# Two mixture-of-experts layers: six weight chunks in flight instead of three, and another order of the expert products

## The chip, the core and the metric

The kernel runs on one core of a Trainium2 chip. The metric is the device time of one execution in microseconds; lower is better. TensorE (PE) multiplies, ScalarE (ACT) and VectorE (DVE) move and transform results, GpSimd (POOL) does one kind of subtraction, and SyncE (SP) issues the loads from device memory (HBM) into the on-chip memory (SBUF). Matmul results land in eight banks of PSUM, here the tensor `bank`.

## What is computed

A model of 256 tokens, 1024 wide: two first blocks (stick-breaking attention or retention, each followed by a mixture-of-experts layer), then a second block (state-space and sparse attention, then a layer that picks from 16384 small experts), all in float32. The change concerns the two mixture-of-experts layers and the weights that they stream:

```python
def grouped_moe(h, router_w, router_b, w_gate, w_up, w_down):
    ...
    for e in range(N_EXPERTS):                       # 16 experts
        hidden = jax.nn.silu(t @ w_gate[e]) * (t @ w_up[e])      # 1024 -> 512
        out = out + combine[:, e:e + 1] * (hidden @ w_down[e])   # 512 -> 1024
```

`combine` is zero except for the two experts that the router chose for a token.

## The kernel before

**Weights.** All weights of the first two blocks and of the mixer lie in one HBM tensor `stream`, in chunks of 128 x 4096 float32 (2 MB). SP loads them in order into `K.ring`, three places (`RING = 3`): chunk n goes to place n % 3, and its load waits until TensorE has used chunk n - 3, counted by the semaphore `chunk_used`. A landed chunk counts on `landed[place]`. SP works through its waits and loads strictly in the order of the program, so each load waits behind the one before it.

**An expert layer** (`moe_stage`, used twice, called `moe0` and `moe1` here) takes two experts, a pair, at a time: 8 pairs, 6 chunks each, 48 chunks a layer. Of the six, two hold the gate weights, two the up weights, two the down weights. At the beginning the layer routes the tokens and gathers each expert's tokens (up to 64) into `slots` with a product by a 0/1 matrix `hot`; `gather(0)` makes the slots of experts 0 to 7, `gather(1)` those of 8 to 15, and `turn_hot` transposes `hot` for the way back. A branch on the router's counts leads to this path (`tensor_gathered`) or to `tensor_dense`; the execution profiled takes the gathered path.

**TensorE's order** in the gathered path: `gather(0)`; gate product of pair 0; `spread_weights`; up product of pair 0; a small product for the output gate; `gather(1)`; `turn_hot`; `turn_hidden(0)`; down product of pair 0. Then for each pair p from 1 to 7: gate product (2 chunks), up product (2 chunks), `scatter` of pair p - 1, `turn_hidden(p)`, down product (2 chunks). At the end `scatter` of pair 7.

**Its partners.** ACT applies Silu to the gate product (bank 4) once both gate chunks are done (`silu_gate`); DVE multiplies it with the up product (bank 5) into `hidden_s` (`make_hidden`); TensorE transposes that into bank 4 (`turn_hidden`); ACT copies it to `hidT` (`take_hidden`), and the down product (banks 6 and 7) waits for the copy. DVE and ACT then split the down product into two parts, `y_hi` and `y_lo` (`split_values`, `take_values`), which `scatter` adds into banks 0 to 3. `y_hi` and `y_lo` lie in `K.halves`, where the tokens' two parts for the gathers had been.

**Other memory.** `K.w_hi` and `K.w_lo` (16 KB a partition each) hold split weights in the retention stage between the two layers; within the expert layers they are idle until the last pair. All instructions of the first products have one line in the profile, L1053; the down products L1094, the gathers L1036, `turn_hot` L1072, `turn_hidden` L1080, `scatter` L1102, SP's chunk loads L1373 in the layers and L149 elsewhere.

## Time and profile before

| | us |
|---|---|
| median of 3 runs | 2084.95 (2083.53 to 2085.63) |
| profiled execution, its own time | 2082.98 |
| its span in the trace | 2081.1 |
| TensorE busy | 1915.7 (92%) |
| weight loads of TensorE busy | 1418.1 (68%) |
| DVE / ACT / POOL busy | 1099.6 / 745.0 / 628.9 |
| read from HBM | 483.41 MB, mean 233 GB/s |

The profiled execution's own time is 1.88 us above its span and 1.97 us below the median of the runs. The busy share of TensorE is an average over stages: matmuls overlap in the pipeline and a stage that waits for its weights stands beside stages that wait for nothing. What decides is, within a stage, which wait ends last.

### The profile page before, as it was taken

How to read it: one execution, taken by the hardware profiler on the slowest of the kernel's cores; microseconds unless marked ns; L12 is line 12 of the kernel's file. 1: busy time of each engine (PE TensorE's matmuls, PEld its weight loads, DVE VectorE, ACT ScalarE, POOL GpSimd, SP SyncE). 2: the span in 40 equal slices, each digit the busy share in tenths (PEclk: the TensorE clock that was granted, in tenths of full speed). 3: DMA queues.
4: the chain of work that ended last, by engine and by line, in shares of the span. 5: the costliest groups of instructions: out<-in, count | busy, mean ns of one | idle time of the engine just before them, and what ended most of it. 6: DMA issues, size and time to landing. Idle time of an engine off the chain costs nothing. (4 is left out here: it accounts for less than half of the span.)

```text
span 2081.1 us, 30590 instructions
## 1 busy us (share of the span) xinstructions
PE 1915.7 (92%) x10508; PEld 1418.1 (68%) x10508; DVE 1099.6 (53%) x2221; ACT 745.0 (36%) x1260; POOL 628.9 (30%) x438
## 2 busy tenths in 40 slices
PE   4989888888999998887999999999999999999998
PEld 4875432237877642222776559999999998888886
DVE  4377210124668621012697521999577776555555
ACT  5362200014354220001512333555544445444444
POOL 6720000016668100000300025898766760000000
PEclk9999999999999899999999999999999999999999
DMA  9874699993668369999332332555444446555554
GB/s 395 311 278 170 242 426 424 427 418 130 230 231 342 123 248 425 413 422 422 106 131 92 132 122 99 174 183 183 162 144 142 144 142 202 191 192 188 190 190 148
DMA packets 76621, 485.54 MB, mean 233 GB/s; under 512 B 9472, under 2 KB 9984, under 8 KB 58624
## 3 DMA queue, kind: packets, MB, share of 16 engines
q1 hardware_dynamic: 75824, 482.88, 61.8%
q10 hardware_dynamic: 720, 1.61, 0.2%
q8 instruction: 50, 0.82, 0.2%
q14 instruction: 27, 0.22, 0.0%
HBM read 483.41 MB, written 1.05 MB: 233 GB/s over the span
## 5 line engine op out<-in xcount | busy, mean ns | idle before, releaser
L3083 POOL TENSOR_TENSOR peer_u_lo<-peer_u,peer_u_hi 128x512 fp32r<-128x512 f32 x255 | 328.2, 1299 | 93.7 <-ACT peer_u_hi L3109 92.1
L3021 PE MATMUL bank<-peer_hn_hi,peer_u_hi 128*128 128x256 f32 x1024 | 294.3, 287 | 3.5 <-ACTq L3096 3.5
L1053 PE MATMUL bank<-ring,moe_slots 128*64 128x512 f32 x1024 | 237.4, 608 | 64.4 <-DMA ring<-in_stream 64.4
L3022 PE MATMUL bank<-peer_hn_lo,peer_u_hi 128*128 128x256 f32 x1024 | 286.6, 280 | 0.0
L3023 PE MATMUL bank<-peer_hn_hi,peer_u_lo 128*128 128x256 f32 x1024 | 286.2, 279 | 0.0
L1053 PEld LDWEIGHTS bank<-ring,moe_slots 128*64 128x64 f32 x1024 | 69.9, 139 | 228.7 <-issue 116.2
L3109 ACT ACTIVATE peer_u_hi<-peer_u 128x512 fp32r<-128x512 f32 x253 | 159.1, 629 | 114.9 <-PE bank L3023 111.2
L3021 PEld LDWEIGHTS bank<-peer_hn_hi,peer_u_hi 128*128 128x128 f32 x1024 | 193.4, 189 | 5.8 <-issue 3.7
L3022 PEld LDWEIGHTS bank<-peer_hn_lo,peer_u_hi 128*128 128x128 f32 x1024 | 193.5, 189 | 0.0
L3023 PEld LDWEIGHTS bank<-peer_hn_hi,peer_u_lo 128*128 128x128 f32 x1024 | 193.2, 189 | 0.0
L217 POOL TENSOR_TENSOR w_lo<-ring,w_hi 128x1024 fp32r<-128x1024 f32 x60 | 148.6, 2478 | 62.7 <-ACT w_hi L207 62.4
L3239 DVE TENSOR_TENSOR peer_v_lo<-peer_scores,peer_v_hi 128x1024 fp32r<-128x1024 f32 x86 | 105.4, 1225 | 102.0 <-ACT peer_v_hi L3129 102.0
L1193 DVE SCALAR_TENSOR_TENSOR moe_hidden_s<-bank,moe_slot_w,moe_gated_s 128x512 f32<-128x512 f32 x16 | 12.0, 749 | 242.7 <-PE bank L1053 242.7
L3129 ACT ACTIVATE peer_v_hi<-peer_scores 128x1024 fp32r<-128x1024 f32 x86 | 91.2, 1061 | 118.6 <-PE bank L3063 112.0
L1094 PE MATMUL bank<-ring,moe_hidT 128*64 128x512 f32 x512 | 117.0, 610 | 14.4 <-ACT moe_hidT L1155 9.6
L3063 PE MATMUL bank<-peer_hn_hi,peer_hn_lo 128*128 128x512 f32 x504 | 121.4, 390 | 0.0
L3063 PEld LDWEIGHTS bank<-peer_hn_hi,peer_hn_lo 128*128 128x128 f32 x504 | 94.6, 188 | 19.6
L1386 POOL TENSOR_TENSOR w_lo<-ring,w_hi 128x1024 fp32r<-128x1024 f32 x4 | 9.5, 2429 | 312.1 <-ACT w_hi L1137 312.1
L322 DVE CUSTOM_DVE_ANT_0 mod<-sb_mod_ring,bank 128x1024 bf16<-128x1024 f32 x64 | 76.7, 1217 | 49.8 <-DMA sb_mod_ring<-in_ada_t 29.3
L207 ACT ACTIVATE w_hi<-ring 128x1024 fp32r<-128x1024 f32 x60 | 63.6, 1060 | 107.2 <-PE bank L246 73.0
L3063 PE MATMUL bank<-peer_v_hi,peer_hn_lo 128*128 128x512 f32 x344 | 100.5, 393 | 0.0
L2044 POOL COPY s_steps<-consts 128x128 f32<-128x128 f32 x1 | 0.3, 293 | 317.9 <-POOLq L115 317.9
(510 smaller groups left out, 3977.8 us busy)
## 6 DMA issues: line engine op xcount, KB each, us to landing
ring<-in_stream SPq DMA_DIRECT2D x135, 2048.0 KB, 10.5
peer_u<-in_peer_u SPq DMA_DIRECT2D x128, 512.0 KB, 3.3
peer_scores<-in_peer_v SPq DMA_DIRECT2D x86, 512.0 KB, 3.3
sb_mod_ring<-in_ada_t SPq DMA_DIRECT2D x64, 512.0 KB, 6.7
peer_u<-in_peer_v SPq DMA_DIRECT2D x42, 512.0 KB, 3.3
ret_mod_ring<-in_ada_t SPq DMA_DIRECT2D x32, 512.0 KB, 5.0
s_bz<-in_b_channel SPq DMA_DIRECT2D x4, 512.0 KB, 6.0
ring<-in_stream SPq DMA_DIRECT2D x2, 1024.0 KB, 5.0
```

Of the source, the lines that this page charges most:

```text
L217: pool.tensor_tensor(self.shaped(self.w_lo, q, by_columns), self.quarter(n, q, by_columns), self.shaped(self.w_hi, q, by_columns).bitcast( ...
L322: dve.tensor_tensor_reduce(out=self.junk[:, b % 2, :], in0=self.ring[:, b % self.slots, :], in1=c_wide, scale=1.0, scalar=0.0, op0=ALU.mul ...
L1053: last = pe.matmul(K.bank[own(e), 4 + up, :], slots[:, f, own(2 * p + e)], w[:, e, k, :], start=(f == 0), stop=(f == KD - 1))
L1094: last = pe.matmul(K.bank[own(e), 6 + dh, :], hidT[:, k, own(e)], w[:, e, k, :], start=(k == 0), stop=(k == 3))
L3021: pe.matmul(out, u_hi[:, b, k2, :], h_hi[:, k, :], start=(k == 0), stop=False)
L3022: pe.matmul(out, u_hi[:, b, k2, :], h_lo[:, k, :], start=False, stop=False)
L3023: last = pe.matmul(out, u_lo[:, b, k2, :], h_hi[:, k, :], start=False, stop=(k == KD - 1))
L3063: last = pe.matmul(K.bank[:, 4 + 2 * tt + dh, :], h[b][:, mine], w[b][:, dh * 512:(dh + 1) * 512], start=first_tile and begins, stop=last_ ...
L3083: pool.tensor_tensor(u_lo[:, b, :, :], u[:, i, KD // 2 * half:KD // 2 * (half + 1), :], u_hi[:, b, :, :].bitcast(F32), ALU.subtract).then_ ...
L3109: act.activation(u_hi[:, b, :, :], u[:, i, KD // 2 * half:KD // 2 * (half + 1), :], ACT.Copy).then_inc(hi_made, 1)
L3129: act.activation(v_hi[i], v[i], ACT.Copy).then_inc(v_ready, 1)
L3239: dve.tensor_tensor(v_lo[i], v[i], v_hi[i].bitcast(F32), ALU.subtract)
```

## The change

The six chunks of a pair get six places. `RING` becomes 4, and in the expert layers two more places, `early`, lie in the memory of `K.w_hi` and `K.w_lo`. Up chunks and (but for the first and last pair) down chunks go through the ring, gate chunks through `early`; the gate chunks of pair 0 come through the ring and the down chunks of pair 7 through `early`. The host lays the chunks out in the order of their use, and `ROW` maps chunk numbers to rows of `stream`. Four chunks of a layer can be in the ring before it begins, and two more are issued as SP's first act in it, ahead of the two rows `g_row` and `b_row`; 42 loads are left for the loop instead of 45. TensorE runs the gate product of pair p + 1 ahead of the down product of pair p, with the transposes of `hidden_s` (now into bank 5) between its two chunks, and `gather(1)` and `turn_hot` come after the up product of pair 1. `y_hi` and `y_lo` get memory of their own. ACT's and DVE's orders follow. The dense path is rewritten for the same chunk order (left out below). A smaller scratch area for GpSimd's loads makes room, and `peer_gap` keeps later buffers off the ring's fourth place.

```diff
--- before.py
+++ after.py
...
-RING = 3
+RING = 4
...
-STREAM = [("sb_in", 6), ("sb_out", 2), ("moe0", 3 * EXPERTS), ("ret_in", 12), ("ret_out", 4), ("moe1", 3 * EXPERTS),
+STREAM = [("sb_in", 6), ("sb_out", 2), ("moe0", 4 * PAIRS), ("ret_in", 12), ("ret_out", 4), ("moe1", 4 * PAIRS),
...
+ROW = []
+_r = 0
+for _name, _count in STREAM:
+    if _name.startswith("moe"):
+        ROW += [_r + 6 * p + m for p in range(PAIRS) for m in range(4)]
+        _r += 6 * PAIRS
+    else:
+        ROW += list(range(_r, _r + _count))
+        _r += _count
+ROWS = _r
...
-        sp.dma_start(K.ring[:, n % RING, 0:size], K.A["stream"][n, :, 0:size]).then_inc(K.landed[n % RING], 16)
+        sp.dma_start(K.ring[:, n % RING, 0:size], K.A["stream"][ROW[n], :, 0:size]).then_inc(K.landed[n % RING], 16)
...
 def weight_buffers(K, scope):
 
+    with ExitStack() as chunks:
+        K.early = chunks.enter_context(K.nc.sbuf_tensor("early", [P, 2, CHUNK], F32))
     K.w_hi, K.w_lo = (scope.enter_context(K.nc.sbuf_tensor(n, [P, 4, CHUNK // 4], F32R)) for n in ("w_hi", "w_lo"))
...
-        y_hi, y_lo = (K.halves[:, 0, i * D:(i + 1) * D] for i in range(2))
+        y_hi, y_lo = (sb(n, [P, D], F32R) for n in ("y_hi", "y_lo"))
...
+        early = [K.early[:, m, :] for m in range(2)]
+        early_landed, early_used = [s_(f"early_in{m}") for m in range(2)], s_("early_used")
+        row0, turn0 = ROW[n0], n0 // RING
+        assert n0 % RING == 0 and n_end % RING == 0
...
+        def chunk(pe, slot, turn):
+
+            pe.wait_ge(K.landed[slot], 16 * (turn + 1) + 16 * turn0)
+            return two_experts(K.ring[:, slot, :])
+
+        def early_chunk(pe, m, turn):
+
+            pe.wait_ge(early_landed[m], 16 * (turn + 1))
+            return two_experts(early[m])
+
+        def gate_chunk(pe, p, m):
+            return chunk(pe, m, 0) if isinstance(p, int) and p == 0 else early_chunk(pe, m, p - 1)
+
+        def down_chunk(pe, p, dh):
+            return early_chunk(pe, dh, PAIRS - 1) if isinstance(p, int) and p == PAIRS - 1 else chunk(pe, dh, p + 1)
+
+        def gate_used(p):
+            return K.chunk_used if isinstance(p, int) and p == 0 else early_used
+
+        def down_used(p):
+            return early_used if isinstance(p, int) and p == PAIRS - 1 else K.chunk_used
+
+        def gated_by(p):
+            return (K.chunk_used, n0 + 2) if isinstance(p, int) and p == 0 else (early_used, 2 * p)
+
+        def downed_by(p, dh):
+            return (early_used, 2 * PAIRS - 1 + dh) if p == PAIRS - 1 else (K.chunk_used, n0 + 4 * p + 5 + dh)
...
+            def gate_product(p, m):
+
+                if p and m == 0:
+                    pe.wait_ge(silu_done, p)
+                first_products(gate_chunk(pe, p, m), p, 0, m).then_inc(gate_used(p), 1)
+
+            def up_product(p):
 
                 for m in range(2):
-                    n = at(p, 2 * up + m)
-                    wait_chunk(pe, K, n)
-                    w = K.ring[:, n % RING, :].rearrange("p (e k c) -> p e k c", e=2, k=4)
-                    for k in range(4):
-                        f = 4 * m + k
-                        if not up and p == 0:
-                            took(0, f)
-                        if not up and p == PAIRS // 2:
-                            took(1, f)
-                        for e in range(2):
-                            last = pe.matmul(K.bank[own(e), 4 + up, :], slots[:, f, own(2 * p + e)], w[:, e, k, :], start=(f == 0),
-                                             stop=(f == KD - 1))
-                    last.then_inc(K.chunk_used, 1)
+                    first_products(chunk(pe, 2 + m, p), p, 1, m).then_inc(K.chunk_used, 1)
...
-                    last = pe.transpose(K.bank[:, 4, k * P:(k + 1) * P], hidden_s[:, k * P:(k + 1) * P], K.ident)
+                    last = pe.transpose(K.bank[:, 5, k * P:(k + 1) * P], hidden_s[:, k * P:(k + 1) * P], K.ident)
...
             gather(0)
             took(0, 2)
-            first_products(0, 0)
+            gate_product(0, 0)
+            gate_product(0, 1)
             spread_weights()
-            first_products(0, 1)
+            up_product(0)
             pe.wait_ge(slot_taken, 2)
             gate.tensor(pe)
+            gate_product(1, 0)
+            turn_hidden(0)
+            gate_product(1, 1)
+            pe.wait_ge(gate.taken, 2)
+            down_product(0)
+            up_product(1)
             gather(1)
             turn_hot()
-            turn_hidden(0)
-            pe.wait_ge(gate.taken, 2)
-            down_product(0)
-            for p in range(1, PAIRS):
-                first_products(p, 0)
-                first_products(p, 1)
-                if p == 1:
-                    pe.wait_ge(copied, 4)
+            gate_product(2, 0)
+            turn_hidden(1)
+            gate_product(2, 1)
+            pe.wait_ge(copied, 4)
+            scatter(0)
+            down_product(1)
+            for p in range(2, PAIRS):
+                up_product(p)
+                if p + 1 < PAIRS:
+                    gate_product(p + 1, 0)
+                turn_hidden(p)
+                if p + 1 < PAIRS:
+                    gate_product(p + 1, 1)
                 scatter(p - 1)
-                turn_hidden(p)
                 down_product(p)
             scatter(PAIRS - 1)
...
+                act.wait_ge(early_used, 2 * PAIRS)
...
-                act.activation(hidT[:].rearrange("p k s -> p (k s)"), K.bank[:, 4, :], ACT.Copy).then_inc(hid_taken, 1)
+                act.activation(hidT[:].rearrange("p k s -> p (k s)"), K.bank[:, 5, :], ACT.Copy).then_inc(hid_taken, 1)
...
+            take_hidden(0)
+            silu_gate(1)
+            take_values(0)
             take_slots(1)
             act.wait_ge(made, 1)
             for b in range(4):
                 act.activation(hotT[:, 2 * b:2 * b + 2, :].rearrange("p a t -> p (a t)"), K.bank[:, b, :], ACT.Copy).then_inc(copied, 1)
-            take_hidden(0)
-            for p in range(1, PAIRS):
+            take_hidden(1)
+            silu_gate(2)
+            for p in range(2, PAIRS):
                 take_values(p - 1)
-                silu_gate(p)
                 take_hidden(p)
+                if p + 1 < PAIRS:
+                    silu_gate(p + 1)
             take_values(PAIRS - 1)
...
                 dve.tensor_copy(slot_w[own(e), :], weights[own(e), :, e]).then_inc(slot_taken, 1)
             dve.wait_ge(slot_taken, 2)
-            take_slots(1)
             make_hidden(0)
...
-            for p in range(1, PAIRS):
+            split_values(0)
+            make_hidden(1)
+            take_slots(1)
+            for p in range(2, PAIRS):
                 split_values(p - 1)
                 make_hidden(p)
...
+                for m in range(2):
+                    sp.dma_start(early[m], K.A["stream"][row0 + 4 + m]).then_inc(early_landed[m], 16)
                 affine_rows(sp, K, 2 * layer, g_row, b_row, rows_in)
-                LOOPS = (n_end - n0 - RING) // RING
-                assert K.fetched == n0 + RING and (n_end - n0) % RING == 0
-                with sp.Fori(0, LOOPS) as i:
-                    for j in range(RING):
-                        slot = (n0 + j) % RING
-                        sp.wait_ge(K.chunk_used, RING * i + (n0 + j + 1))
-                        sp.dma_start(K.ring[:, slot, :], K.A["stream"][RING * i + (n0 + RING + j)]).then_inc(K.landed[slot], 16)
+                assert K.fetched == n0 + RING
+                with sp.Fori(0, PAIRS - 1) as i:
+                    for slot in range(RING):
+                        sp.wait_ge(K.chunk_used, RING * i + (n0 + slot + 1))
+                        sp.dma_start(K.ring[:, slot, :], K.A["stream"][6 * i + (row0 + 6 + slot)]).then_inc(K.landed[slot], 16)
+                    for m in range(2):
+                        sp.wait_ge(early_used, 2 * i + (m + 1))
+                        sp.dma_start(early[m], K.A["stream"][6 * i + (row0 + 10 + m)]).then_inc(early_landed[m], 16)
                 K.fetched = n_end
...
+            peer.enter_context(nc.sbuf_tensor("peer_gap", [P, CHUNK], F32))
...
-    return parts
+    gates, ups, downs = parts[0::3], parts[1::3], parts[2::3]
+    order = [gates[0], ups[0], gates[1]]
+    for p in range(PAIRS):
+        order += [downs[p]] + ups[p + 1:p + 2] + gates[p + 2:p + 3]
+    return order
...
-    nc = bacc.Bacc("TRN2", target_bir_lowering=False, num_devices=1)
+    nc = bacc.Bacc("TRN2", target_bir_lowering=False, num_devices=1, dynamic_dma_scratch_size=1024)
```

TensorE, from `gather(0)` of the first layer to the first `scatter`; `ring` and `early` are the chunk places, `moe_slots` the gathered tokens, `moe_hot` the 0/1 matrix. Before:

```order
L1036 MATMUL bank<-moe_hot,halves 128x512 x32
L1053 MATMUL bank<-ring,moe_slots 64x512 x16
L1062 MATMUL bank<-moe_comb,moe_hot 128x2 x16
L1053 MATMUL bank<-ring,moe_slots 64x512 x16
L356 MATMUL bank<-mod,consts 128x512 x2
L1036 MATMUL bank<-moe_hot,halves 128x512 x32
L1072 MATMUL bank<-consts,moe_hot 128x128 x16
L1080 MATMUL bank<-consts,moe_hidden_s 128x128 x4
L1094 MATMUL bank<-ring,moe_hidT 64x512 x16
L1053 MATMUL bank<-ring,moe_slots 64x512 x32
L1102 MATMUL bank<-halves,moe_hotT 128x512 x8
```

The same stretch of the changed kernel, whose line numbers are other ones (L1081 gathers, L1094 first products, L1144 down products):

```order
L1094 MATMUL bank<-ring,moe_slots 64x512 x16
L368 MATMUL bank<-mod,consts 128x512 x2
L1094 MATMUL bank<-early,moe_slots 64x512 x8
L1132 MATMUL bank<-consts,moe_hidden_s 128x128 x4
L1094 MATMUL bank<-early,moe_slots 64x512 x8
L1144 MATMUL bank<-ring,moe_hidT 64x512 x16
L1094 MATMUL bank<-ring,moe_slots 64x512 x16
L1081 MATMUL bank<-moe_hot,halves 128x512 x32
L1124 MATMUL bank<-consts,moe_hot 128x128 x16
L1094 MATMUL bank<-early,moe_slots 64x512 x8
L1132 MATMUL bank<-consts,moe_hidden_s 128x128 x4
```

Six more chunks' products (two gate, two down, two up) now stand between the first up product and the second gather. One `order` row of x16 is two chunks, of x8 one chunk.

SP in the first layer, from its first load there to the end of its loop. Before:

```order
L522 DMA mod<-in_ln_g 128x1024
L523 DMA moe_b_row<-in_ln_b 128x1024
L1369 UNCONDITIONAL_BRANCH
L1369 ISA
L1373 ISA
L1373 DMA ring<-in_stream 128x4096
L1372 REGISTER_ALU
L1373 ISA
L1373 DMA ring<-in_stream 128x4096
L1373 ISA
L1373 DMA ring<-in_stream 128x4096
```

Of the changed kernel, the loads ahead of the loop and the last of its body, with the loads for the next stage behind it:

```order
L1433 DMA early<-in_stream 128x4096 x2
L534 DMA mod<-in_ln_g 128x1024
L535 DMA moe_b_row<-in_ln_b 128x1024
...
L1442 DMA early<-in_stream 128x4096
L1441 REGISTER_ALU
L1442 ISA
L1442 DMA early<-in_stream 128x4096
L1436 REGISTER_ALU
L1436 COMPARE_AND_BRANCH
L159 DMA ring<-in_stream 128x4096 x4
```

Two chunk loads stand ahead of the two rows, the loop's body has six chunk loads instead of three, and the next stage's first loads are four instead of three.

## Rows read from the trace of the kernel before

**Rows 1.** The page: the span, and DMA's busy tenths and rate in 40 slices.

```profile
span 2081.1 us, 30590 instructions
...
DMA  9874699993668369999332332555444446555554
GB/s 395 311 278 170 242 426 424 427 418 130 230 231 342 123 248 425 413 422 422 106 131 92 132 122 99 174 183 183 162 144 142 144 142 202 191 192 188 190 190 148
```

**Rows 2.** Both expert layers: stretch, its length, busy times, granted clock, DMA share, GB/s.

```profile
208.79:461.91 253.12, 212.77 (x950) 81.54 (x950) 39.82 (x75) 30.02 (x54) 0.95 (x1) 0.98 0.93 389
730.09:983.74 253.65, 211.40 (x949) 80.13 (x948) 39.34 (x72) 29.33 (x52) 0.00 (x0) 0.99 0.93 388
```

**Rows 3.** TensorE's waits in the first layer (208 to 462): total, times, longest.

```profile
PE bank L1053 <- DMA ring<-in_stream: 31.4, 26, 2.4
PE bank L1094 <- ACT moe_hidT L1155: 4.8, 7, 0.7
```

**Rows 4.** TensorE's timeline, one pair: start, duration, [idle before <- releaser].

```profile
300.47 2.11 PE L1102 MATMUL bank<-halves,moe_hotT 128*128 128x512 f32 x8
302.43 0.60 PE L1080 MATMUL bank<-consts,moe_hidden_s 128*128 128x128 f32 x4
303.71 7.09 PE L1094 MATMUL bank<-ring,moe_hidT 128*64 128x512 f32 x32 [0.69 <-ACT moe_hidT L1155]
311.58 3.65 PE L1053 MATMUL bank<-ring,moe_slots 128*64 128x512 f32 x16 [0.79 <-DMA ring<-in_stream]
316.47 3.65 PE L1053 MATMUL bank<-ring,moe_slots 128*64 128x512 f32 x16 [1.23 <-DMA ring<-in_stream]
...
329.84 2.11 PE L1102 MATMUL bank<-halves,moe_hotT 128*128 128x512 f32 x8
```

**Rows 5.** Stretches of both layers' beginning and rest, columns as rows 2.

```profile
236.00:249.00 13.00, 9.87 (x47) 5.43 (x48) 8.08 (x24) 3.15 (x6) 0.00 (x0) 0.87 0.04 19
249.00:252.00 3.00, 3.00 (x16) 1.21 (x14) 1.06 (x3) 0.60 (x1) 0.00 (x0) 1.00 0.81 224
252.00:455.00 203.00, 166.79 (x742) 58.03 (x740) 23.28 (x33) 16.13 (x27) 0.00 (x0) 0.99 1.01 426
...
757.00:768.00 11.00, 7.87 (x40) 4.04 (x40) 6.71 (x18) 2.55 (x5) 0.00 (x0) 0.84 0.00 1
...
771.00:976.00 205.00, 166.90 (x742) 57.73 (x739) 23.32 (x33) 16.13 (x27) 0.00 (x0) 0.99 1.00 420
```

**Rows 6.** TensorE's timeline at the beginning of the first layer.

```profile
208.79 7.09 PE L1053 MATMUL bank<-ring,moe_slots 128*64 128x512 f32 x32
215.81 3.73 PE L1062 MATMUL bank<-moe_comb,moe_hot 128*128 128x2 f32 x32
219.47 8.78 PE L1053 MATMUL bank<-ring,moe_slots 128*64 128x512 f32 x32
...
229.61 8.02 PE L1036 MATMUL bank<-moe_hot,halves 128*128 128x512 f32 x32
...
240.27 0.60 PE L1080 MATMUL bank<-consts,moe_hidden_s 128*128 128x128 f32 x4
243.13 8.79 PE L1094 MATMUL bank<-ring,moe_hidT 128*64 128x512 f32 x32 [2.25 <-issue]
```

**Rows 7.** SP's timeline, two chunk loads; then landing times of 205 to 260.

```profile
212.63 0.35 SPq L1373 DMA_DIRECT2D ring<-in_stream  x1
...
248.66 0.33 SPq L1373 DMA_DIRECT2D ring<-in_stream  x1
...
DMA to landing us min/median/max: 7.5/9.0/12.0
```

**Rows 8.** SP's first load in the layer, and the stretch ahead of its first chunk load.

```profile
189.70 0.33 SPq L522 DMA_DIRECT2D mod<-in_ln_g  x1
...
196.00:213.00 17.00, 16.90 (x62) 10.15 (x63) 8.50 (x19) 6.01 (x13) 0.00 (x0) 0.80 0.00 0
```

**Rows 9.** TensorE's timeline at the end of the first layer.

```profile
444.64 3.65 PE L1053 MATMUL bank<-ring,moe_slots 128*64 128x512 f32 x16 [1.24 <-DMA ring<-in_stream]
...
458.48 1.21 PE L1102 MATMUL bank<-halves,moe_hotT 128*128 128x512 f32 x4
460.70 1.21 PE L1102 MATMUL bank<-halves,moe_hotT 128*128 128x512 f32 x4 [1.02 <-DVE halves L1204]
```

More of the change, by code:

```diff
@@ L1327, in make_hidden @@
             def make_hidden(p, first=False):
-                dve.wait_ge(K.chunk_used, 6 * p + (n0 + 4))
+                dve.wait_ge(K.chunk_used, 4 * p + (n0 + 4))
                 dve.wait_ge(silu_done, 4 * p + 4)
-                if not first:
-                    dve.wait_ge(K.chunk_used, 6 * p + n0)
                 for b in range(4):
```

95 lines of the change are left out of this document (51 added, 44 removed).

## The prediction

> **What bounds the kernel now.** I read the page's slices first, to find where the loads are at their limit. Two stretches of four to five slices run at 413 to 427 GB/s with DMA at 9 tenths; the rest is lower, mostly 90 to 250, with 395 in the kernel's first slice [rows 1]. These two are the expert layers. The second view is the busy time of each layer: 253.1 and 253.7 us long, of which TensorE is busy 212.8 and 211.4, DVE under 40, ACT under 31 [rows 2]. So TensorE idles 40 to 42 us in each, and the list of waits names the cause: 31.4 us of the first layer for a chunk that has not landed, 26 times, and 4.8 us for ACT's copy of the transposed hidden rows [rows 3].
>
> The timeline of one pair shows the rhythm: from one scatter to the next 29.37 us (300.47 to 329.84) for six chunks, 4.9 us each, with 1.23 us of waiting before a product of 3.65 us [rows 4]. TensorE's own work in that pair is 4 x 3.65 + 7.09 + 2.11 + 0.60 = 24.4 us. Loads are the bound, and they run at their limit: DMA share 1.01 and 426 GB/s from 252 to 455 [rows 5]; 2.097 MB / 426 GB/s = 4.92 us. I take 4.9.
>
> But not everywhere. From 236 to 249 the share is 0.04, with a ramp up to 252; in the second layer it is 0.00 from 757 to 768 [rows 5]. The beginning of the layer shows why. The three chunks present at 208.79 are used up by 224; the loads that replace them are in by about 235; the gather and the turning of `hot` hold TensorE from 229.6 to 240.3, and the next place comes free only in the down product that starts at 243.13 [rows 6]. SP's next load is issued at 248.66 [rows 7]. Before that, ahead of the first chunk load at 212.63, DMA is idle for 17 us with a share of 0.00 [rows 8].
>
> **The change, part by part.** *Six places instead of three.* 45 loads were left when the first place came free; now 42. The two `early` loads are issued where the two rows are now, at 189.7; they take 9.8 us and the rows move behind them. DMA has nothing from 196 to 213 [rows 8], so the loads cost nothing; the rows, wanted by DVE only behind the first hidden product (after 228), come about 10 us later than now, which is cover enough. If the cover were gone DVE would hold up the first down split, at worst by those 10 us once a layer.
>
> *The new order.* I walk through the first layer with today's durations. Up to the end of the small product at 229.6 nothing moves. Then gate chunk (3.65) to 233.3, transposes (0.6) to 233.9, gate chunk to 237.5, down product of pair 0 (7.1) to 244.6, up product of pair 1 (7.3) to 251.9, gather and turning (229.61 to 240.27, so 10.7) to 262.6, gate chunk to 266.2. Places come free at 212.4, 215.9, about 224, 228.2, 233.3, 237.5, 241.1, 244.6, 248.3, 251.9 and then 266.2. Ten loads can therefore follow one another from about 214.2 (1.6 us from issue to flow; landings here take 7.5 to 12.0 us, median 9.0, so 2.6 to 4.1 us around the flow of 4.9, of which I put 1.6 ahead and 2 behind [rows 7]). A hole of 1.7 us around 224 exists today too. Ten loads end at 214.2 + 1.7 + 49 = 265. The eleventh flows at 268: one hole of 3 us takes the place of today's. Behind it TensorE, at 24.4 us a pair, frees places faster than 29.4 us a pair fills them, so DMA never idles again, and from about the fifth pair TensorE waits for each chunk as now. The last load is through at 268 + 32 x 4.9 = 424.8. Then 2 us to land, one chunk's product, 3.65, and the scatter with its wait, 3.43 (458.48 to 461.91) [rows 9]: the layer ends at 433.9.
>
> The same sum for the kernel before: the fifth load flows at 250.3, 41 loads to 451.2, plus 9.1 gives 460.3 where the trace has 461.9. So the method is 1.6 us short, and the gain is 26.4 by the sum, 28.0 against the trace; I take 27. It splits into 14.7 us for three loads fewer and about 12 for the hole that shrinks from some 14 us (13 x 0.96 plus the ramp) to 3. The second layer has 11 us at 0.00 and a shorter ramp [rows 5], so I take 26 there.
>
> *What is hidden.* Silu of pair p + 1 is asked for one product later than now, but its reader, the next gate product's bank, is wanted a whole up product later. ACT's copy of the hidden rows (0.69 us of wait per pair [rows 4]) lies under the second gate chunk; this frees TensorE, not DMA, so it is worth nothing where loads are the bound, and it stays a wait only for pair 7, whose scatter now covers it. DVE's splits gain a product of slack. The new order needs no more matmuls; the separate `y_hi` and `y_lo` remove a conflict and cost nothing.
>
> *Elsewhere.* `RING = 4` lets the other stages run one chunk further ahead. Their DMA is at 3 to 8 tenths [rows 1]; a fourth prefetched chunk puts the loads behind it back by 4.9 us at a stage's start. The tail of a layer to the next stage's first own load is over 19 us, four chunks. I take zero, bounded by -3 (an earlier chunk helps somewhere) and +5 us (one chunk's delay exposed at the start of the kernel, where DMA is at 9 tenths).
>
> **Sum.** 27 + 26 = 53 us off the profiled execution's 2082.98, so 2030.0; the median of the runs is 1.97 above that execution, so 2032.
>
> **A rule against the trace.** The waits of 1.23 us repeat before every chunk for 200 us while DMA's share is 1.01 [rows 4, 5]. More places cannot remove a wait for a channel that is never idle; only the hole and the three loads count. The Trainium skill (Perfetto Trace Analysis, Optimization Strategy) reads a gap that repeats on the engine that should be saturated as a possible lack of room for the next tile. By that rule all waits would go, the first rival below; by the share it won't.
>
> **Rivals.**
> 1. *All waits for chunks go.* The layer would run at TensorE's pace: with the walk above and 24.4 us a pair it ends near 421 instead of 434, 41 us less than now; twice that gives 2003. Against it: 42 loads of 4.9 us from 214 alone end at 420, and the product behind the last is still to come, so it needs loads faster than any stretch shows. 4%.
> 2. *The hole stays.* If a wait I have not seen (the splits of pair 0 behind DVE's 16 row pieces, or the rows that now arrive later) holds the down product of pair 0 or the second gather back by 10 us, only the three loads are saved: 15 a layer, 2055. For it: DVE is busy 8.1 of 13 us just there [rows 5]. 10%.
> 3. *A new small wait per pair*, say TensorE at the head of its longer queue (gate chunk of p + 1 not landed while the down product could run). Loads come in the order of use, so it costs only while TensorE is behind; 3 to 8 us a layer, 2038 to 2048. 4%.
> 4. *No net change*: the four prefetched chunks delay the next stage as much as the layer gains. It would need 25 us where 4.9 is the size of the effect. 3%.
> 5. *Slower: the clock.* TensorE's granted clock is 0.98 and 0.99 of full over the layers, and 0.87 or 0.84 in the thin stretch of the gathers [rows 2, 5]. Now 212 us of work stand in 226 instead of 253. If the chip answered the denser work with the lower level, 1.2 instead of 2.4 GHz, for part of it, the layer would become TensorE's: the point is a mean of 212/253 = 0.84, below which it is slower than now; at 0.8 it is 265 us, 12 more a layer, 2109. Against it: the low stretches follow thin work, not dense. 3%. The Trainium skill (TensorE: Matmul & The Clock Gate, HAM oscillation) says the same, that idling for loads is what throttles, and by it this rival falls away.
>
> My own case has 76%, with 2024 to 2040 for it: the hole may close entirely (3 us a layer, 2026), landing may cost 1 to 2 us more or less, and the other stages give -3 to +5.
>
> **Numbers.** The likeliest is 2032. The range reaches from 2022 to 2050: it takes in my case and rival 3 and leaves rivals 1, 4, 5 and most of 2 outside. A measurement of this kernel tells a change from none at about 0.2%, 4 us. Faster: 76 + 4 + 10 + 4 = 94%; the same 3%; slower 3%.
>
> **What the profile after would show.** The layers 226 to 228 us long with TensorE's busy time unchanged near 212; one DMA hole of about 3 us near 265 instead of 13 near 240; the time from the first loop load to the last one's landing about 213 us; waits for chunks of 1.2 us only from the fifth pair on, 10 to 14 us in all instead of 31; no wait of TensorE for ACT's hidden copy; landing times of 20 us and more, since up to five loads queue, without any product waiting longer for it. The retention stage's beginning and everything behind the second layer should keep its length within 3 us. The forecast is wrong if the pair's period stays at 29.4 from the second pair on (rival 2), if it falls below 25 to the end (rival 1), or if the clock in the layer falls below 0.9.

## The result, and the profile after

The changed kernel takes 2028.31 us (median of 4 runs, 2027.39 to 2030.75) against 2084.81 us (4 runs, 2083.53 to 2085.63): a ratio of 0.9731 with a 95% interval of 0.9714 to 0.9748, 56.5 us less. The span of the profiled execution falls from 2081.1 to 2027.0 us, 54.1 less. The forecast was 2032 us.

The page's slices of the changed kernel, to be laid beside [rows 1]:

```profile
span 2027.0 us, 30581 instructions
...
DMA  9876799984678499997333223555444446555554
GB/s 394 354 292 253 310 408 430 430 346 169 241 262 306 187 410 404 429 430 293 120 109 135 84 104 105 185 180 184 151 140 145 143 151 202 188 193 188 192 190 145
```

The two stretches above 400 GB/s (the expert layers) are shorter, and what stands behind them runs at much the same rates as before. The windows of the two layers, columns as in [rows 2]:

```profile
208.95:436.71 227.76, 210.36 (x950) 81.08 (x950) 39.94 (x75) 30.13 (x54) 0.95 (x1) 0.99 0.97 406
705.20:930.35 225.15, 207.05 (x949) 79.66 (x948) 39.45 (x72) 29.42 (x52) 0.00 (x0) 1.00 0.98 411
```

The layers were 253.12 and 253.65 us long and are 25.4 and 28.5 us shorter, 53.9 of the 54.1 us of the span. TensorE's busy time is 2.4 and 4.4 us less, its granted clock is 0.99 and 1.00, and DMA's share rose from 0.93 to 0.97 and 0.98. The waits of TensorE in the first layer (208 to 437), to be compared with [rows 3]:

```profile
PE bank L1094 <- DMA ring<-in_stream: 7.8, 7, 1.2
PE bank L1094 <- DMA early<-in_stream: 5.3, 6, 1.3
PE bank L1144 <- DMA ring<-in_stream: 1.5, 3, 0.5
PE bank L1152 <- DVE moe_y_lo L1271: 1.0, 1, 1.0
PE bank L1124 <- DVE moe_slots L1252: 0.9, 1, 0.9
PE bank L1132 <- DVE moe_hidden_s L1260: 0.9, 1, 0.9
```

14.6 us for chunks where 31.4 were, none for ACT's hidden copy, and one new wait of 0.9 us: L1132 (`turn_hidden` of pair 7) for DVE's hidden product. Stretches of the first layer, to be compared with [rows 5]:

```profile
225.00:230.00 5.00, 5.00 (x23) 1.39 (x19) 0.00 (x0) 0.00 (x0) 0.00 (x0) 0.92 0.46 128
230.00:265.00 35.00, 34.12 (x160) 15.93 (x160) 12.91 (x30) 7.02 (x13) 0.00 (x0) 1.00 1.01 430
265.00:275.00 10.00, 10.00 (x48) 3.98 (x46) 0.00 (x0) 2.21 (x5) 0.00 (x0) 1.00 0.89 341
275.00:425.00 150.00, 134.50 (x607) 47.31 (x604) 21.21 (x30) 13.61 (x23) 0.00 (x0) 1.00 1.01 428
```

The hole of 236 to 252 is gone. Two dents are left, stretches in which DMA runs below its full rate: 225 to 230 and 265 to 275. SP's timeline says when places come free, since each load goes out as its place does; one row holds the loads of one loop body in a row (`x4` into the ring, `x2` into `early`):

```profile
190.36 0.80 SPq L1433 DMA_DIRECT2D early<-in_stream  x2
...
212.82 17.74 SPq L1439 DMA_DIRECT2D ring<-in_stream  x4
235.72 4.50 SPq L1442 DMA_DIRECT2D early<-in_stream  x2
243.34 10.62 SPq L1439 DMA_DIRECT2D ring<-in_stream  x4
267.69 4.50 SPq L1442 DMA_DIRECT2D early<-in_stream  x2
277.50 10.62 SPq L1439 DMA_DIRECT2D ring<-in_stream  x4
```

The loads are numbered from 212.82 on: the 11th goes out at 267.69, the 13th at 277.50, of 42. The reader should keep these two times.

TensorE's timeline of the changed kernel: the up product of pair 0, the second gather, what stands behind it, one product of each kind in the pairs that TensorE paces (pair 3's and pair 4's gate chunks, 23.53 us apart), and the first wait for a chunk:

```profile
220.15 9.89 PE L1094 MATMUL bank<-ring,moe_slots 128*64 128x512 f32 x32
...
253.37 7.73 PE L1081 MATMUL bank<-moe_hot,halves 128*128 128x512 f32 x32
...
263.85 3.65 PE L1094 MATMUL bank<-early,moe_slots 128*64 128x512 f32 x16
...
273.64 7.09 PE L1144 MATMUL bank<-ring,moe_hidT 128*64 128x512 f32 x32
...
287.43 3.60 PE L1094 MATMUL bank<-early,moe_slots 128*64 128x512 f32 x16
...
310.96 3.60 PE L1094 MATMUL bank<-early,moe_slots 128*64 128x512 f32 x16
...
331.61 3.65 PE L1094 MATMUL bank<-ring,moe_slots 128*64 128x512 f32 x16 [0.38 <-DMA ring<-in_stream]
```

### The profile page after: what moved, and what is told of

Its sections match the earlier page's. It is cut to its first block and busy times, and to the rows that moved or that the text cites. A ratio compares the mean times of both kernels' runs of the same rounds, so it can differ in the third digit from the quotient of the medians.

```text
span 2027.0 us, 30581 instructions
## 1 busy us (share of the span) xinstructions
PE 1904.9 (94%) x10508; PEld 1414.0 (70%) x10508; DVE 1096.4 (54%) x2221; ACT 745.1 (37%) x1260; POOL 628.2 (31%) x438
## 5 line engine op out<-in xcount | busy, mean ns | idle before, releaser
L1094 PE MATMUL bank<-ring,moe_slots 128*64 128x512 f32 x576 | 131.7, 606 | 16.3 <-DMA ring<-in_stream 16.3
L1269 DVE TENSOR_TENSOR bank<-bank,mod 128x512 f32<-128x512 f32 x32 | 22.4, 700 | 220.3 <-PE bank L1144 220.3
L1094 PEld LDWEIGHTS bank<-ring,moe_slots 128*64 128x64 f32 x576 | 40.4, 139 | 103.5 <-issue 73.9
L1094 PE MATMUL bank<-early,moe_slots 128*64 128x512 f32 x448 | 102.1, 597 | 10.7 <-DMA early<-in_stream 10.7
L1144 PE MATMUL bank<-ring,moe_hidT 128*64 128x512 f32 x448 | 100.4, 596 | 3.0 <-DMA ring<-in_stream 3.0
## 6 DMA issues: line engine op xcount, KB each, us to landing
early<-in_stream SPq DMA_DIRECT2D x32, 2048.0 KB, 19.4
```

What stands on the lines that cost most here:

```text
L1094: last = pe.matmul(K.bank[own(e), 4 + up, :], slots[:, f, own(2 * p + e)], w[:, e, k, :], start=(f == 0), stop=(f == KD - 1))
L1144: last = pe.matmul(K.bank[own(e), 6 + dh, :], hidT[:, k, own(e)], w[:, e, k, :], start=(k == 0), stop=(k == 3))
```

## The experiments

Ten other kernels ran, and the changed one a second time. Experiments 1, 2, 5 and 7 ran first, then 3, 4 and 6; on these a theory fell and another was formed, and 8 to 10 test it. The edits are shown against the changed kernel and cut; where the order of products moves, ACT's and DVE's orders follow. The times of before beside them were 2083.9 to 2085.3 us.

**1. Six places alone.** The stream's rows, the order of products and the gather as before; gates and ups in the ring, downs in `early` (the loop's body is cut: the first `scatter` waits for the copies of the turned matrix, as before):

```
             gather(1); turn_hot(); turn_hidden(0); down_product(0)
             for p in range(1, PAIRS):
                 gate_product(p, 0); gate_product(p, 1); up_product(p)
                 scatter(p - 1); turn_hidden(p); down_product(p)
```

> Six places and the two loads issued at the layer's start, but the kernel before's order of products (gate, up, down of a pair, the stream in that order) and its early gather. Theory (the gain is 42 loads in place of 45 at 4.9 us, and whatever the DMA hole gives back): u0b is used at about 230, the four loads that it and the three chunks ahead of it release are through at about 235, the next place comes free with the first half of down product 0 at about 247, so a hole of 11 to 13 us a layer stays where the changed kernel has some 4. So about 8 us a layer more than the changed kernel: 2028 + 16 = 2044 us (2040 to 2048), layers of 235 us. Rival A (the order of the products brings the gain, since the waits for ScalarE and VectorE go with it): 2065 us or more. Rival B (the places do it all, the late gather hides nothing): 2028 to 2032 us.

2047.69 us (2047.12 to 2049.88), ratio 0.9821 (0.9796 to 0.9846); layers of 237.0 and 237.2 us. As the theory said, if a little more (8 us a layer expected, 9.2 and 12.1 measured). The places alone bring 36 of the 56 us.

**2. The gather early, all else as changed.**

```
             gate.tensor(pe)
+            gather(1)
+            turn_hot()
             gate_product(1, 0)
```

> The changed kernel with the second gather and the turns of the one-hot matrix put back ahead of the second gate product, as they stood before. Theory (places come free only with a used chunk, so 12 us of gather and turns that use none leave the queue without work): the four loads of the first pair are through at about 235, the next place comes free at about 246; a hole of 11 us in place of two small ones of together 4: plus 7 us a layer, 2042 us (2038 to 2046). Rival (the waits for chunks at the layer's end are set by PE's pace, and the place of the gather is of no account): 2026 to 2031 us.

2044.52 us (2044.01 to 2045.99), ratio 0.9805 (0.9780 to 0.9829); 7.6 us more in each layer, as expected. The window 238 to 246 of this kernel:

```profile
238.00:246.00 8.00, 7.13 (x42) 3.62 (x42) 7.19 (x22) 2.75 (x6) 0.00 (x0) 1.00 0.00 0
```

TensorE works 7.13 of 8 us and uses no chunk, so DMA stands at 0.00.

**3. The old order of products, the gather late.** As experiment 1, with `gather(1)` and `turn_hot()` behind `up_product(1)`.

> The changed kernel with the old order of products and of the stream (gate, up, down of a pair), so that only the six places and the late second gather are kept, the gather after the up product of pair 1. Theory (what counts is when places come free, not which product stands where): the waits of TensorE for the hidden values come back, 0.7 to 1 us a pair, but in the stretch that the loads set they lie inside the wait for the next chunk; 0 to +3 us, 2028 to 2031 us. Rival (the gate product in front of the down product is worth a wait for ScalarE and VectorE in each pair, 8 pairs x 2 layers x 1 us): 2040 us or more.

2041.43 us (2041.05 to 2042.81), ratio 0.9792 (0.9774 to 0.9810). My theory missed by 11 us and the rival's number came true. The trace shows where; two rows of TensorE's timeline behind the gather, cut off at 272:

```profile
265.55 0.79 PE L1152 MATMUL bank<-moe_y_hi,moe_hotT 128*128 128x512 f32 x1 [2.15 <-ACT moe_hotT L1225]
...
270.29 1.94 PE L1144 MATMUL bank<-early,moe_hidT 128*64 128x512 f32 x8 [0.69 <-ACT moe_hidT L1208]
```

and the window 260 to 275:

```profile
260.00:275.00 15.00, 11.28 (x53) 6.55 (x53) 1.39 (x2) 3.22 (x7) 0.00 (x0) 0.89 0.50 212
```

In the old order the turned matrix is followed by a wait of 2.15 us for its copies, the scatter and the hidden rows; no chunk is used till the down product at 270.29, and SP's 11th load goes out at 274.13. In the changed kernel a gate product stands there. The rival's number, but for the larger part not its mechanism, as experiment 8 shows.

**4. The gather one product later still**, behind `gate_product(2, 1)`.

> The changed kernel with the second gather and the turns moved one product further back, behind the gate product of pair 2. Theory (the hole in the DMA at 266 to 270 us goes, since two more places come free ahead of the gather; the next, the first half of down product 1, comes at about 273, when 12 loads are just through): minus 1.6 us a layer, 2025 us (2023 to 2028). Rival (the wait for the copies of the one-hot matrix now stands open ahead of the first scatter, and the waits for chunks take nothing back): 2028 to 2032 us.

2030.15 us (2026.80 to 2032.48), ratio 0.9737 (0.9718 to 0.9755): no difference from the changed kernel. The theory (2025) missed, the rival (2028 to 2032) came true. The 11th load goes out early, but the gather now stands ahead of the 13th, with the copies' wait open in front of the scatter:

```profile
269.30 0.50 PE L1152 MATMUL bank<-moe_y_hi,moe_hotT 128*128 128x512 f32 x1 [2.16 <-ACT moe_hotT L1236]
```

The 13th goes out 69.0 us after the layer's first product, 68.6 in the changed kernel. The hole moved.

**5. No head start.** The two `early` loads at the layer's start wait for the first used chunk; the two rows go out ahead of them.

```
+                sp.wait_ge(K.chunk_used, n0 + 1)
                 for m in range(2):
                     sp.dma_start(early[m], ...)
```

> The changed kernel, but its two loads that go out at the layer's start (some 20 us ahead of the first used chunk) wait for the first used chunk of the layer, in front of the loop's own; nothing else is changed. Theory (the loads of a layer after its first used chunk set its end): 44 loads in place of 42 are 9.8 us a layer, less the holes that the two now fill (4 us in the first layer, 1.6 us in the second): plus 5.5 and 8 us, 2041 us (2038 to 2048). Rival (TensorE's own work sets the layer's end, and six places hide two late loads): 2026 to 2031 us.

2035.43 us (2034.95 to 2036.07), ratio 0.9760 (0.9736 to 0.9784). Slower by 7.1 us, less than the 13 expected. The two loads count, but not at 4.9 us each; the bounds in the table below say why.

**6. Three uses ahead.** Six places, but loads wait for the chunk three back in the order of use:

```
-                        sp.wait_ge(K.chunk_used, RING * i + (n0 + slot + 1))
+                        used, count = ((K.chunk_used, RING * i + (n0 + 4)), (early_used, 2 * i + 1),
+                                       (early_used, 2 * i + 2), (K.chunk_used, RING * i + (n0 + 5)))[slot]
+                        sp.wait_ge(used, count)
...
-                        sp.wait_ge(early_used, 2 * i + (m + 1))
+                        sp.wait_ge(K.chunk_used, RING * i + (n0 + 6 + m))
```

> The changed kernel, with all six places and the head start, but each load of the loop waits until the chunk three back in the order of use is used, as with three places; the first six chunks still lie ready. Theory (places are a stock: it matters when loads may begin, not that each is six uses ahead in the steady stretch): the loop's first load begins at about 230 instead of 213 us, 17 us later, of which the holes of the changed kernel (4 us and 1.6 us) come off: plus 13 and 15 us, 2056 us (2050 to 2062), and the steady pairs keep their 29.3 us. Rival (three uses ahead are too few to keep the queue filled, each load then shows some of its latency): the steady pairs take over 30.5 us, and the time is 2070 us or more.

2067.70 us (2064.98 to 2069.67), ratio 0.9918 (0.9896 to 0.9941): slower than expected by 12 us, so both numbers miss. The steady pairs, however, run nearly as in the changed kernel, 29.48 us from one up product to the next (there 29.24), against the rival (TensorE's timeline, cut off at 342):

```profile
312.23 3.65 PE L1094 MATMUL bank<-ring,moe_slots 128*64 128x512 f32 x16 [1.24 <-DMA ring<-in_stream]
...
341.71 0.65 PE L1094 MATMUL bank<-ring,moe_slots 128*64 128x512 f32 x2 [1.23 <-DMA ring<-in_stream]
```

Its window 262 to 275:

```profile
262.00:275.00 13.00, 13.00 (x68) 6.14 (x70) 0.00 (x0) 3.26 (x6) 0.00 (x0) 1.00 0.54 199
```

The loss lies around the gather, where the hole of the first kernel is back (0.54 and 199 GB/s).

**7. Shorter loads.** The ring's 28 loads of a layer bring three quarters of a chunk; this kernel leaves out a quarter of those weights, and its output is not the reference's. TensorE's work is the same.

```
+SHORT_LOAD = 3072
-                        sp.dma_start(K.ring[:, slot, :], K.A["stream"][...])
+                        sp.dma_start(K.ring[:, slot, 0:SHORT_LOAD], K.A["stream"][..., 0:SHORT_LOAD])
```

> The changed kernel, but the loop's loads into the four ring places move only 3072 of their 4096 columns (1.5 MB for 2 MB); the products read the whole place, so a quarter of those weights is stale and the output is not the reference's. TensorE does the same work. Theory (the loads bound the layer from the fifth pair on): 28 loads of 3.7 and 14 of 4.9 us are 172 us of transfers after the first used chunk in place of 206, so the waits for chunks go, 7.8 + 5.3 + 1.5 us in the first layer and 8.5 + 5.4 + 1.5 us in the second, and the layers end at TensorE's pace of 23.5 us a pair: plus perhaps 1 us of other waits left, 2028 - 27 = 2001 us (1998 to 2006). Rival (those waits are a latency of the queue or of the landing and come back with any size): 2020 us or more. Rival (a TensorE without waits gets a lower granted clock): over 2030 us.

1994.35 us (1991.94 to 1995.18), ratio 0.9558 (0.9534 to 0.9582). No wait for a chunk is left in either layer, and they take 208.4 and 210.0 us. The window 275 to 400:

```profile
275.00:400.00 125.00, 125.00 (x576) 45.24 (x574) 19.76 (x28) 13.10 (x22) 0.00 (x0) 1.00 1.01 425
```

TensorE is busy 125 of 125 us at full clock, 1.00. So the waits belonged to the bytes, and no loss of clock comes with an unbroken stretch of work. DMA still runs at 425 GB/s. A pair's shorter loads are 10.5 MB, which at that rate is 24.7 us (an estimate) against TensorE's 23.5, so here too the loads are a little slower; the stock of six places covers the difference to the layer's end (the ring's loads landed after 8.6 us at 277.8 and after 14.8 at 382.2).

It is 7 us faster than I had expected. The layers fell by 19.4 and 15.1 us, where the listed waits for chunks are 14.6 and 15.3. But the openings of the layers differ: the 11th load went out 1.6 us earlier in the first layer than in the changed kernel's profile and 3.4 us later in the second (the clock, last section). With that taken out both layers fell by 3.2 us more than the waits listed, over 16 waits each: a product that stops for a chunk loses about 0.2 us beside the listed wait. One pair of the changed kernel says the same: from 385.21 to 414.45 it takes 29.24 us with 4.8 us of waits listed (1.24 + 1.24 + 1.27 + 0.52 + 0.49), while it is 5.7 longer than 23.53.

**The new theory.** Load n can't go out before its place is free, and those behind it follow at 4.9 us each. So the loads of a layer end at the *latest* of the bounds

t(n) + (loads from the n-th on) x 4.9 us,

with t(n) the time from the layer's first gate product to SP's n-th load, taken from each trace. Holes don't add up; the worst bound counts. In the steady stretch a place comes free only because an earlier load has landed, so there every n gives about the same sum (n = 35 gives 241.2 in the kernel before); only the bounds ahead of that stretch explain anything. For the changed kernel t(1) = 3.9 gives 3.9 + 42 x 4.9 = 209.7, t(11) = 58.7 gives 58.7 + 32 x 4.9 = 215.5, t(13) = 68.6 gives 68.6 + 147 = 215.6. The gather makes the 11th and 13th the worst. Three kernels were built on it, and the changed kernel ran once more beside them.

> The changed kernel itself, for a comparison beside the three kernels of this batch, whose expected differences are small: 2028 us (2026 to 2031).

2028.51 us (2024.50 to 2031.47), ratio 0.9724 (0.9710 to 0.9738).

**8. The scatter ahead of the gate product of pair 2.**

```
+            pe.wait_ge(copied, 4)
+            scatter(0)
             gate_product(2, 0)
             turn_hidden(1)
             gate_product(2, 1)
-            pe.wait_ge(copied, 4)
-            scatter(0)
```

> The changed kernel, but the wait for the copies of the turned one-hot matrix and the scatter of pair 0 stand ahead of the gate product of pair 2, not behind it; everything else as in the changed kernel. It asks why six places with a late gather in the old order of products took 2041 us. Theory, formed on that run (a layer's loads end at the latest of: the moment of its n-th used chunk, plus the loads from the n-th on at 4.9 us; the gather makes the eleventh to thirteenth the latest, and what stands right behind the gather counts in full): the wait of 2.2 us and the scatter of 2 us now come ahead of the eleventh used chunk, which ends at 271.9 us in place of 267.5; plus 4.4 us a layer, 2037 us (2034 to 2040). Rival (the order of products brought its 13 us by the waits for ScalarE and VectorE in every pair, which this kernel hides as the changed one does): 2028 to 2031 us.

2037.22 us (2034.93 to 2039.92), ratio 0.9771 (0.9756 to 0.9786): slower by 8.7 us, as expected. The order of products in every pair is the changed kernel's, so most of experiment 3's 13 us (8.7 of them) comes from what stands behind the gather, not from the waits in each pair. The window 262 to 275 of this kernel:

```profile
262.00:275.00 13.00, 11.55 (x54) 4.80 (x56) 0.00 (x0) 2.59 (x5) 0.00 (x0) 1.00 0.58 229
```

**9. The weights spread later.**

```
-            spread_weights()
             up_product(0)
-            pe.wait_ge(slot_taken, 2)
-            gate.tensor(pe)
+            spread_weights()
             gate_product(1, 0)
+            pe.wait_ge(slot_taken, 2)
+            gate.tensor(pe)
```

> The changed kernel with the 4 us of products that spread the weights moved from ahead of the up product of pair 0 to behind it, and the gate row behind the first half of gate product 1. The third and fourth used chunks come 4 us earlier, and the hole in the DMA at 222 to 230 us shrinks. Theory (the latest of the bounds counts, not the sum of the holes): the eleventh used chunk stays at 267.5 us, since TensorE does the same work ahead of it, so the hole only moves there; 2028 us (2026 to 2030). Rival (the holes add up): 4 us in the first layer and 1 to 2 us in the second go, 2022 to 2024 us.

2028.49 us (2028.24 to 2030.59), ratio 0.9727 (0.9714 to 0.9740): nothing gained, and the rival (holes add up, 2022 to 2024) is out. The first dent is filled and the second deeper. Two windows of this kernel, then the same two of the changed kernel's second run:

```profile
222.00:232.00 10.00, 10.00 (x54) 5.25 (x50) 5.03 (x16) 0.00 (x0) 0.00 (x0) 0.83 1.02 433
262.00:275.00 13.00, 13.00 (x60) 5.02 (x60) 0.00 (x0) 3.26 (x6) 0.00 (x0) 1.00 0.80 306
...
222.00:232.00 10.00, 10.00 (x44) 3.36 (x42) 6.25 (x19) 1.48 (x3) 0.00 (x0) 1.00 0.88 344
262.00:275.00 13.00, 13.00 (x62) 5.11 (x60) 1.39 (x2) 1.79 (x3) 0.00 (x0) 1.00 0.91 350
```

**10. The gather split.** As 9, but only four of the gather's eight pieces stay behind the up product of pair 1; two go behind that of pair 2 and two behind that of pair 3:

```
-            gather(1)
+            gather(1, range(4))
             turn_hot()
 ...
                 up_product(p)
+                if p in (2, 3):
+                    gather(1, range(2 * p, 2 * p + 2))   # banks 6, 7
```

> The kernel with the weights spread later, and of the second gather only four of its eight pieces stand behind the up product of pair 1; two stand behind the up product of pair 2 and two behind that of pair 3, in the banks of the down product. Theory (the latest of the bounds): 3.9 us of gather leave the stretch ahead of the eleventh and thirteenth used chunk, whose bounds fall from 424.3 to 420.4 us, with the first at 418.6 and the fourth at 417 us; minus 3.9 us a layer, 2020 us (2018 to 2024), faster than the changed kernel. Rival (the waits for the banks and for the copies of the later pieces stand open, or the pairs that TensorE paces get 2 us longer and the loads catch nothing): 2027 to 2032 us.

2022.03 us (2020.33 to 2025.21), ratio 0.9695 (0.9682 to 0.9708), 6.5 us below the changed kernel beside it, and the intervals of the ratios don't meet. The 11th load goes out 53.1 us after the layer's first product (at 210.86), against 58.7 and 57.1 in the two profiles of the changed kernel. SP's row that begins with it, and two windows:

```profile
263.94 4.50 SPq L1451 DMA_DIRECT2D early<-in_stream  x2
...
222.00:232.00 10.00, 10.00 (x58) 5.56 (x56) 3.35 (x11) 0.00 (x0) 0.00 (x0) 0.87 1.02 433
262.00:275.00 13.00, 13.00 (x62) 4.98 (x59) 0.74 (x2) 2.06 (x4) 0.00 (x0) 1.00 1.00 413
```

Both dents are closed. This version beats both kernels. Here t(1) gives 209.7, t(11) and t(13) 209.9 and t(6) 210.3, so by the bounds another order is worth at most 0.6 us in this layer, and a further gain needs another stock of chunks at the start; no kernel tried that.

The worst bound against the measured first layer, all in us, from each kernel's SP timeline:

| kernel | worst bound | layer | difference |
|---|---|---|---|
| before | t(5) 39.9 + 41 x 4.9 = 240.8 | 253.1 | 12.3 |
| places alone | t(5) 39.9 + 38 x 4.9 = 226.1 | 237.0 | 10.9 |
| gather early | t(5) 37.1 + 38 x 4.9 = 223.3 | 235.4 | 12.1 |
| old order, gather late | t(11) 64.6 + 32 x 4.9 = 221.4 | 232.4 | 11.0 |
| three ahead | t(10) 71.6 + 33 x 4.9 = 233.3 | 245.9 | 12.6 |
| no head start | t(1) 3.7 + 44 x 4.9 = 219.3 | 230.2 | 10.9 |
| scatter first | t(11) 61.4 + 32 x 4.9 = 218.2 | 230.4 | 12.2 |
| changed | t(13) 68.6 + 30 x 4.9 = 215.6 | 227.8 | 12.2 |
| changed, second time | t(11) 57.1 + 32 x 4.9 = 213.9 | 226.1 | 12.2 |
| gather later | t(13) 69.0 + 30 x 4.9 = 216.0 | 226.8 | 10.8 |
| spread later | t(11) 56.8 + 32 x 4.9 = 213.6 | 225.3 | 11.7 |
| split gather | t(6) 29.0 + 37 x 4.9 = 210.3 | 222.3 | 12.0 |

Over 31 us of layer length the difference stays between 10.8 and 12.6. In each of the twelve the last of the loop's chunks landed 3.0 to 4.9 us behind the bound, and the layer ended 7.5 to 7.8 us behind that landing, with the last product and the last scatter (428.97 and 436.71 in the changed kernel). In the second layers, which the table leaves out, the same sum leaves 10.7 to 12.9 us, and 14.6 in the kernel before, whose loads were slower there (next section). Experiment 5 comes out too: its bound is 3.7 us above the changed kernel's, and it took 7.1 us more in two layers. The theory was formed on the kernels of experiments 1 to 7 and the times t(n) are read from the traces, so of the table only the last three experiments are a test: 8, 9 and 10 came out at 2037.22, 2028.49 and 2022.03 us for 2037, 2028 and 2020.

## Why the prediction was right, step by step

*The loads bind, 4.9 us a chunk at full rate*: right. Shown by experiment 7 (fewer bytes, no waits) and by 428 GB/s from 275 to 425.

*42 loads for 45 and a hole that shrinks, 27 + 26 us*: right in the sum (53 forecast, 53.9 measured in the layers). By the worst bound of the first layer, 240.8 - 215.6 = 25.2 us: three loads are 14.7 and the rest is 10.5.

*The walk through the opening*: nearly right. It had the eleventh place free at 266.2; it came at 267.7. The step behind it, that TensorE at 24.4 us a pair "frees places faster than 29.4 us a pair fills them, so DMA never idles again", failed: the 12th and 13th places need the second gate chunk, the scatter and half a down product, 9.8 us for two, which is just the loads' own pace. The bound of the 13th is as high as that of the 11th. (TensorE's own pair took 23.53 us: the forecast added up durations whose ends overlap what follows. That was worth nothing.)

*One hole of 3 us, and 1.7 us at 224*: the size was off, and the sum of holes is the wrong account. I measured idle DMA by its share. Where one load ends and the next has only begun the share is 0.46 to 0.89 but the rate 128 to 341 GB/s; by the rate, (429 - 284) / 429 x 17 us from 213 to 230 and (429 - 395) / 429 x 25 us from 250 to 275 are 5.7 (1.2 of them ahead of 214.2, where the forecast's flow begins) and 2.0 us. But filling the first dent gained nothing (experiment 9), so that is not where the miss comes from.

*The first layer ends at 433.9*: it ended at 436.7. The 11th place came 1.5 us late, since the up product of pair 0 took 9.89 us for 8.78 and the weights' products 4.25 for 3.73. The rest is the end: the last chunk landed 4.5 us behind the bound where 1.6 + 2 were allowed, and the layer ended 7.7 us behind that where 7.1 were. The sum for the kernel before was itself 1.6 us short, as the forecast says.

*27 and 26*: 25.4 and 28.5, so which layer gains more came out the other way, and the close total is in part luck: two misses of opposite sign. The changed kernel's second layer had its up product of pair 0 in 7.09 us where the first layer's took 9.89, and its weights' products in 3.73 for 4.25, so all bounds behind them lie 3.3 us lower (the 11th place frees 55.2 us after the first product for 58.6). In its second run it was the other way round: 9.88 us in the second layer, and layers of 226.1 and 227.8. And the kernel before had the short product in its second layer too (t(5) is 38.1 for 39.9) and was still the longer one: its loads ran at 420 GB/s there for 426 in the first layer [rows 5], 2.9 us over the 205 us, while the changed kernel has 427 and 428. Why they were slower in that stretch stays open.

*Landing times of 20 us and more without harm*: 18.1 at the median, 25.4 at most, and no product waits for more than 1.3 us. The waits for chunks begin with the fifth pair, as forecast (331.61), and are 14.6 us for the 10 to 14 expected; the stretch from the first loop load to the last landing is 216.2 us for 213. (The waits of the kernel before do not stand "before every chunk": they are 26 for 45 loads [rows 3].)

*Nothing from the hidden copies*: right; the wait that I had left to pair 7 did not stay with ACT but with DVE (L1132, 0.9 us), since `turn_hidden` of pair 7 has no gate product in front of it.

*Elsewhere 0 (-3 to +5)*: right, 54.1 - 53.9 = 0.2 us (0.2 longer ahead of the first layer, 0.3 longer between the layers, 0.7 shorter behind the second).

*The rivals.* All waits go: no, 14.6 us of them stay in the first layer. The Trainium skill (Perfetto Trace Analysis, Optimization Strategy) reads a repeating gap on the engine that should be saturated as a possible lack of room. Six places for three left gaps of 1.2 us, and the shorter loads of experiment 7 removed them, so this trace disagrees with that reading here. The hole stays, 2055: not with the late gather, but experiments 1 and 2 with an early one landed at 2047.7 and 2044.5, so this was the real danger. A new wait in each pair: no, the only new one is the 0.9 us of pair 7. No net change: no, the other stages moved by 0.2 us. Slower by the clock: no. The granted clock was 0.99 and 1.00 in the layers, and 1.00 in the 125 us of unbroken work of experiment 7. The Trainium skill (TensorE: Matmul & The Clock Gate, HAM oscillation) says that waiting for loads is what throttles. The 125 us without a wait at 1.00 agree with it; the fall to 0.50 in the last section came behind no wait.

What the three parts are worth: places alone 36 us, the order without the late gather 3 more (experiment 2; the two kernels' runs don't overlap, but the intervals of their ratios do), the late gather without the order 6 more (experiment 3), both together 19 more. They don't add, because the worst bound takes another place: t(5) stays the worst with the order alone, t(11) becomes it with the gather alone.

## What to carry to other kernels

When loads run at their full rate and buffers are a ring, write for each load the time at which its place comes free plus all loads that follow; the largest sum sets the end, and only work ahead of that load is worth moving. More places act as a stock that carries over stretches in which no buffer is used up, here the gather; in the steady stretch three ahead ran nearly as well as six (29.48 and 29.24 us a pair). Measure a dent in DMA by its rate, not by its busy share.

## What the runs showed of the hardware

A load that finds an empty queue pays for its start, and loads in a row do not: the one issued at 226.8 in the changed kernel landed after 7.6 us, while the steady stretch takes 4.9 us a load. Waiting in a queue only lengthens the landing: 7.6 to 25.4 us (median 18.1) for the ring's loads of the changed kernel's first layer, 10.0 to 10.9 in the steady stretch with three ahead, at 428 and 427 GB/s. A long time to landing was no cost.

The up product of pair 0 took 9.89 us in the first layer of the changed kernel and 7.09 in the second; in its second run 8.79 and 9.88, for the same 32 products, 16 a chunk. The granted clock shows why:

```profile
203.00:219.00 16.00, 16.00 (x85) 9.74 (x84) 3.59 (x9) 6.12 (x14) 0.00 (x0) 1.00 0.43 163
219.00:225.00 6.00, 6.00 (x19) 2.59 (x20) 0.33 (x2) 0.00 (x0) 0.00 (x0) 0.50 0.91 385
```

TensorE was busy all of the 16 us ahead of 219, and yet the clock was 0.50 from 219 to 225, which is 1.2 of 2.4 GHz. What TensorE did just before and as it fell is the weights' products (`spread_weights`, L1114, 215.97 to 220.22), 32 products of 2 columns each. Experiments 9 and 10 moved them behind the up product, and the fall moved with them. In experiment 9 they run from 223.06 to 226.79:

```profile
219.00:225.00 6.00, 6.00 (x38) 3.09 (x34) 0.00 (x0) 0.00 (x0) 0.00 (x0) 1.00 1.02 434
228.00:231.00 3.00, 3.00 (x8) 0.73 (x6) 3.00 (x11) 0.00 (x0) 0.00 (x0) 0.50 1.01 431
```

The up product then took 7.04 us, and the gate product behind the weights' products 5.35 for 3.65. In 24 of the 26 layers profiled the clock falls within 1.5 us of the end of these products; in the second layers of the kernel before and of the changed kernel it doesn't fall there at all. So the fall follows this thin work, though TensorE counts as busy in it. That it is the cause is likely and not shown, and why the low stretch is longer in some profiles, and missing in two, stays open. It moved the 11th free place by up to 3.3 us between layers of the same kernel, so a difference of that size between single layers says nothing of an edit.
